# Gathered expert rows of a 32-row tile: weighting and adding them on GpSimd instead of DVE

## The chip, the cores and the metric

The kernel runs on one core of one Trainium2 chip. The metric is the device time of one execution in microseconds (us). The engines are named PE (TensorE, the matrix engine), DVE (VectorE), ACT (ScalarE), POOL (GpSimd) and SP (SyncE, here only a queue that starts transfers). DVE and POOL can both do elementwise work on tiles in SBUF; POOL cannot reach PSUM, where PE leaves its sums.

## What is computed

One inference step of a two-layer encoder. There are 288 tokens: 256 of a prompt and 32 of a sample. A layer is attention, a projection, a layer norm, a mixture of 16 experts of which each token uses two, and a second layer norm:

```python
x = layernorm(DN_ALPHA * x + mix, p['ln1_g'][l], p['ln1_b'][l])
ffn = grouped_moe(x, ...)   # y = y + gate[:, e:e + 1] * (h @ w_down[e])
x = layernorm(DN_ALPHA * x + ffn, p['ln2_g'][l], p['ln2_b'][l])
```

The change is in the last line of the second layer: `DN_ALPHA * x + ffn` for the sample's 32 rows. For each token `ffn` is the sum of two expert rows, each times its gate.

## The kernel before

Every engine has its own list of instructions, written out by hand in one function per engine; nothing reorders them. Semaphores are all that joins them: an instruction may wait for a count, and raises another when it is done. A helper `own(...)` raises the engine's own semaphore (or a named one), `own.settle()` waits for the last instruction that it issued, and `step(...)` does both on DVE.

Tokens lie on partitions in three tiles, `TOKS = [(0, P), (P, P), (2 * P, DEC)]`: tile 0 and tile 1 are the prompt (128 rows each), tile 2 is the sample (32 rows). `x_tok[:, t, :]` is tile t of the residual stream, 1024 values of float32 in each row.

In a layer, each expert works on a list of up to 64 tokens. PE multiplies them by the gate and up weights (`expert_up`, L916), DVE and ACT form the hidden values, PE turns them (`expert_turn`, L923) and multiplies by the down weights (`expert_down`, L930). The weights come in from HBM, 6 MB for each expert, through SP's queue. The results of the first 14 experts of the second layer are stored into the DRAM tensor `expert_rows` by ACT's queue (`store`, L1397). POOL's queue brings each token's two rows back with gathers (`bring_back`, L2043): for tile t the rows land in `back[0:n, s, t, :]`, with s = 0 and 1, and `back_in[t]` counts them. The six gathers are issued in the order tile 0, tile 1, tile 2. They start once the store of expert 13 has landed.

The last two experts of the second layer are not stored. ACT copies their results into `y_pair` (`keep`, L1405), and PE adds them to the tiles by a matmul with `pair_t`, a matrix with the tokens' gates. So the second layer ends like this:

- DVE multiplies `x_tok` by ALPHA in expert 14's time (L1868), and after expert 15's `turned` runs through the three tiles (L1934 to L1940). For each of a tile's two gathered rows one `scalar_tensor_tensor` computes `back * pair_gate + x_tok`, six of them in all. The second one of each tile raises `part_ready`.
- PE's `add_tile(l, t)` (L1021) waits for `part_ready` of tile t, puts the tile into PSUM with a matmul by the identity (L1026) and adds the last two experts' share (L1032). It raises `tile_ready`. Tiles 0, 1 and 2 have PSUM banks of their own (`sum_bank`).
- DVE's `combine(t)` (L1912) waits for `tile_ready` and computes the row statistics from PSUM (L1918, L1920), subtracts the mean and multiplies by the gain (L1923); ACT computes the root (L1359); DVE's `ln_finish` (L1725, L1727) multiplies by the inverse root and adds the offset. L1727 reads two tiles in SBUF, as L1939 does; L1923 reads one tile in PSUM and one in SBUF.
- SP stores each finished tile (L624).

The first layer has its own form of `combine` (L1926 to L1932) and ends without `add_tile`.

Of the kernel before, what the change touches and what calls it, by code (L numbers as in the profile page):

```python
# [21 lines left out]
ALU = mybir.AluOpType  # L22
# [4 lines left out]
SEQ, DEC, PAST, MEM = 256, 32, 256, 256  # L27
# [24 lines left out]
ALPHA = (2 * DEPTH) ** 0.25  # L52
# [54 lines left out]
def encoder_step(nc, ins, outs):  # L107
    ctx = ExitStack()
    with ctx:
        def sem(name):  # L110
            return ctx.enter_context(nc.semaphore(name))
# [24 lines left out]
        x_tok = base.cut(3, D)  # L136
# [23 lines left out]
        def cst(name, rows=slice(0, P)):  # L160
            a, n = CONST[name]
            return const[rows, a:a + n]
# [58 lines left out]
        back = Region(gu_one_at).cut(2, 3, D)  # L221
# [47 lines left out]
        pair_gate = zr.cut(2, 3)  # L269
# [45 lines left out]
        y_stored = [sem(f"y_stored{j}") for j in range(2)]  # L315
        back_in = [sem(f"back_in{t}") for t in range(3)]
        pair_ready = sem("pair_ready"); pair_turned = sem("pair_turned"); pair_taken = sem("pair_taken")
        pair_copied = sem("pair_copied"); part_ready = sem("part_ready"); tile_ready = sem("tile_ready")
        OV = ("ov_w", "ov_xg", "ov_gu", "ov_sig", "ov_h", "ov_ht", "ov_htc", "ov_y", "ov_yc", "ov_st", "ov_dve")
        ov = [{n: sem(f"{n}_{l}") for n in OV} for l in range(DEPTH)]  # L320
        out_mem = sem("out_mem"); out_kv = sem("out_kv"); out_dk = sem("out_dk"); out_y = sem("out_y")
# [97 lines left out]
        def pairs(l):  # L419

            return sum(PAIR[:l])

        def sum_bank(t, c):

            return bank[((0, 1), (5, 6), (2, 7))[t][c]]
# [212 lines left out]
        def rows_dst(i):  # L638

            blk, k0 = turns[i]  # L640
            a, n = ROW_BLOCKS[blk]
            return (xs[:, a:a + n, k0:k0 + 4].rearrange("p n k -> p k n"),
                    turn_bank(i)[:, :].rearrange("p (k n) -> p k n", k=4)[:, :, 0:n])
# [6 lines left out]
        def _(pe):  # L650
# [370 lines left out]
            def add_tile(l, t):  # L1021

                a, n = TOKS[t]
                pe.wait_ge(part_ready, 3 * pairs(l) + t + 1)
                for c in range(2):
                    mm(sum_bank(t, c)[0:n, :], ident[0:n, 0:n], x_tok[0:n, t, 512 * c:512 * c + 512], start=True, stop=False)  # L1026
                if t == 0:
                    pe.wait_ge(pair_taken, pairs(l) + 1)
                for c in range(2):
                    if t == 0:  # L1030
                        pe.wait_ge(pair_copied, 4 * pairs(l) + 3 + c)
                    last = mm(sum_bank(t, c)[0:n, :], pair_t[:, a:a + n], y_pair[:, c, :], start=False, stop=True)  # L1032
                last.then_inc(tile_ready, 1)
# [171 lines left out]
            for t in range(3):  # L1205
                add_tile(1, t)
# [289 lines left out]
        def _(ve):  # L1496
            own = Own(ve, dve_own)
            V = nc.vector
            tt, ts, stt, red = V.tensor_tensor, V.tensor_scalar, V.scalar_tensor_tensor, V.tensor_reduce

            def step(ins, s=None):

                own(ins, s)
                own.settle()
# [300 lines left out]
            def hidden(j, s, n, signal):  # L1805

                ts(act[:, j, :], act[:, j, :], 1.0, None, ALU.add).then_inc(s, 1)
                ve.wait_ge(s, n + 1)
                V.reciprocal(act[:, j, :], act[:, j, :]).then_inc(s, 1)
                ve.wait_ge(s, n + 2)  # L1810
                tt(act[:, j, :], act[:, j, :], bank[j][:, 0:256], ALU.mult).then_inc(s, 1)
                ve.wait_ge(s, n + 3)
                tt(hid[:, j, :], act[:, j, :], bank[j][:, 256:512], ALU.mult).then_inc(signal, 1)

            def hidden_t(j, signal):
                V.tensor_copy(hid_t[:, j].rearrange("p c n -> p (c n)"), bank[2][:, 0:256]).then_inc(signal, 1)  # L1816

            def experts(l):
                def form(e):

                    a = act[:, e % 2, :]
                    ve.wait_ge(sig_ready, NE * l + e + 1)
                    step(ts(a, a, 1.0, None, ALU.add))
                    step(V.reciprocal(a, a))  # L1824
                    step(tt(a, a, bank[e % 2][:, 0:256], ALU.mult))
                    own(tt(hid[:, e % 2, :], a, bank[e % 2][:, 256:512], ALU.mult), h_ready)

                def turned(e):
                    ve.wait_ge(ht_ready, NE * l + e + 1)
                    hidden_t(e % 2, ht_copied)  # L1830

                def pair_weights():

                    own(ts(pair_row, row_ab, float(-PAIR_ROW), None, ALU.add))
                    step(ts(pair_keep, row_ab, float(PAIR_ROW), None, ALU.is_ge))
                    step(stt(pair_keep, row_ab, float(ROWS), pair_keep, ALU.is_lt, ALU.mult))
                    step(ts(pair_keep, pair_keep, -1.0, 1.0, ALU.mult, ALU.add))
                    own(tt(row_ab, row_ab, pair_keep, ALU.mult))
                    step(tt(pair_gate, gates, pair_keep, ALU.mult))
                    own(V.tensor_copy(out_row[:, :], row_ab[:, :, :].rearrange("p s t -> p (s t)")))  # L1840
                    for t, (a, n) in enumerate(TOKS):
                        own(ts(pair_hot[0:n, t, :], cst("iota")[0:n], pair_row[0:n, 0, t:t + 1], gates[0:n, 0, t:t + 1],
                               ALU.is_equal, ALU.mult))
                        step(ts(pair_tmp[0:n], cst("iota")[0:n], pair_row[0:n, 1, t:t + 1], gates[0:n, 1, t:t + 1],
                                ALU.is_equal, ALU.mult))
                        step(tt(pair_hot[0:n, t, :], pair_hot[0:n, t, :], pair_tmp[0:n], ALU.add),
                             pair_ready if t == 2 else None)

                form(0)
                turned(0)  # L1850
                form(1)
                for i in range(1, TURNS, 2):
                    ve.wait_ge(rows_turned, TURNS * l + i + 1)
                    V.tensor_copy(*rows_dst(i)).then_inc(rows_taken["v"], 1)
                turned(1)
                form(2)
                for e in range(3, NE):
                    turned(e - 1)
                    form(e)
                    if PAIR[l] and e == 5:  # L1860
                        pair_weights()
                    if PAIR[l] and e == 7:
                        ve.wait_ge(pair_turned, pairs(l) + 1)
                        own(V.tensor_copy(pair_t, bank[5][:, 0:NT]), pair_taken)
                    if e == NE - 2:
                        ve.wait_ge(x_sorted, 96 * (l + 1))
                        for t in range(3):
                            own(ts(x_tok[:, t, :], x_tok[:, t, :], ALPHA, None, ALU.mult))  # L1868
                turned(NE - 1)
                ve.wait_ge(starts_ready, l + 1)  # L1870
                more = ve.value_load(flag[0:1, 0:1], min_val=0, max_val=1)
                with ve.If(more > 0):
                    o = ov[l]
                    with ve.Fori(0, NE) as e:
                        with ve.Fori(0, PASSES - 1) as q:
                            n = (PASSES - 1) * e + q
                            ve.wait_ge(o["ov_sig"], n + 1)
                            hidden(0, o["ov_dve"], 3 * (PASSES - 1) * e + 3 * q, o["ov_h"])
                            ve.wait_ge(o["ov_ht"], n + 1)
                            hidden_t(0, o["ov_htc"])  # L1880

            def after_attention(l):
# [21 lines left out]
                copies(f"xb{l}", lambda k, b: feat_dst(k + 2, b))  # L1904
                route(l)
                experts(l)

                own.settle()
# [23 lines left out]
                    ln_stats(2 * l + 1, t)  # L1932

                if PAIR[l]:  # L1934
                    for t in range(3):
                        n = TOKS[t][1]
                        ve.wait_ge(back_in[t], 32 * (l + 1))
                        for s in range(2):
                            step(stt(x_tok[0:n, t, :], back[0:n, s, t, :], pair_gate[0:n, s, t:t + 1], x_tok[0:n, t, :],  # L1939
                                     ALU.mult, ALU.add), part_ready if s else None)  # L1940
# [43 lines left out]
        def _(po):  # L1984
            own = Own(po, pool_own)
            G = nc.gpsimd
# [30 lines left out]
            def layer(l):  # L2017
# [34 lines left out]
                with po.If(more > 0):  # L2052
                    po.wait_ge(ov[l]["ov_st"], 32 * NE * (PASSES - 1))
                    ln_load(ln2_par, "ln2_g", "ln2_b", l)
                    bring_back(PASSES * ROWS)

            layer(0)
            layer(1)

# [1 line left out]
_INS = ["x_prompt", "x_sample", "cache_mla_ckv", "cache_mla_kpe", "cache_diff_k", "cache_diff_v", "cache_mem_k",  # L2061
# [25 lines left out]
```

## Time and profile before

| what | us |
|---|---|
| median of three runs | 941.51 |
| the three runs | 935.6, 941.51, 945.32 |
| the profiled execution, its own time | 942.3 |
| its span in the trace | 940.5 |
| PE busy | 807.9 (86% of the span) |
| DVE busy | 335.1 (36%) |
| POOL busy | 44.1 (5%), most of it the issuing of transfers |

The time of the profiled execution is 1.8 us above its span. All starts below are counted from the span's start. Shares of the whole span say little on this change: it lies in the last 25 us, so that stretch is what has to be read. Idle time of an engine counts only where the chain of waits runs through it.

### The profile page before, as it was taken

Reading aid. Unit: us, or ns where it says so; the run is one execution under the profiler, and the core shown is the slowest. Engines: PE = TensorE matmul, PEld = TensorE weight load, DVE = VectorE, ACT = ScalarE, POOL = GpSimd, SP = SyncE. Lnnn points to the kernel's source line nnn. Section 1 sums busy time; section 2 is a strip of 40 time slices with the busy share of each in tenths; the row PEclk is TensorE's granted clock in tenths of the full one; section 3 lists DMA queues with packets and bytes.
Section 4 is the critical chain, followed back from the end, with each engine's and each line's share of the span. In section 5 each row is a group of like instructions: output and inputs, shape, how many; then the busy total and the mean of one; then the engine's idle time right before and its main releaser. Section 6 shows DMA issues by size and latency. Waiting matters only on the chain.

```text
span 940.5 us, 10036 instructions
## 1 busy us (share of the span) xinstructions
PE 807.9 (86%) x3983; PEld 402.1 (43%) x3983; DVE 335.1 (36%) x749; ACT 186.5 (20%) x452; POOL 44.1 (5%) x58
## 2 busy tenths in 40 slices
PE   6979999998999887786889888879899998787875
PEld 4665777553433222222334566654544332222221
DVE  1025454444422221213360243454443342212138
ACT  1213343110311111100100034440103211101001
POOL 1012000002000000000200000000020000000020
PEclk9998899999999999998989897989999999999898
DMA  9624006746999999999596330093659999999991
GB/s 353 225 77 180 1 1 265 317 177 240 405 425 425 427 425 427 423 426 425 188 397 229 146 109 1 21 421 140 241 210 411 426 425 428 424 428 420 428 403 61
DMA packets 43553, 272.82 MB, mean 290 GB/s; under 512 B 6360, under 2 KB 11166, under 8 KB 25840
## 3 DMA queue, kind: packets, MB, share of 16 engines
q1 hardware_dynamic: 32032, 243.69, 63.0%
q0 software_dynamic: 5888, 19.95, 6.3%
q10 hardware_dynamic: 5584, 8.51, 2.5%
q8 instruction: 33, 0.54, 0.2%
q14 instruction: 16, 0.13, 0.0%
HBM read 253.92 MB, written 18.21 MB: 289 GB/s over the span
## 4 chain that ended last, share of the span: by engine, by line
PE 53%; DMA 26%; DVE 9%; SPq 6%; ACT 2%; issue 2%; POOL 0%; ACTq 0%; DVEq 0%; POOLq 0%
DMA arena<-in_expert_w_up 24%; PE bank L916 16%; PE bank L858 6%; PE bank L930 5%; PE bank L1176 5%; PE bank L845 3%; SPq L503 2%; PE bank L781 2%; PE bank L833 2%; PE bank L939 1%; PE bank L826 1%; PE bank L678 1%; PE bank L759 1%; PE bank L1141 1%; SPq L499 1%
## 5 line engine op out<-in xcount | busy, mean ns | idle before, releaser
L916 PE MATMUL bank<-arena 128*64 128x512 f32 x1024 | 240.8, 627 | 51.0 <-DMA arena<-in_expert_w_up 49.2
L916 PEld LDWEIGHTS bank<-arena 128*64 128x64 f32 x1024 | 77.2, 144 | 211.5 <-issue 148.2
L930 PE MATMUL bank<-arena 128*64 128x512 f32 x512 | 116.9, 598 | 16.7 <-DVE arena L1816 16.2
L1816 DVE COPY arena<-bank 128x256 f32<-128x256 f32 x32 | 13.6, 424 | 274.7 <-PE bank L923 274.7
L930 PEld LDWEIGHTS bank<-arena 128*64 128x64 f32 x512 | 34.1, 136 | 77.4 <-issue 55.4
L1372 ACT ACTIVATE arena<-bank 128x256 f32<-128x256 f32 x32 | 12.3, 384 | 268.8 <-PE bank L916 268.8
L1824 DVE RECIPROCAL arena<-arena 128x256 f32<-128x256 f32 x32 | 56.1, 1753 | 1.1
L858 PE MATMUL bank<-arena 128*128 128x512 f32 x128 | 56.0, 596 | 0.0
L1176 PE MATMUL bank<-arena 128*128 128x512 f32 x96 | 44.6, 628 | 5.0 <-DMA arena<-in_w_kv_shared 4.2
L845 PE MATMUL bank<-arena 128*128 128x288 f32 x128 | 39.0, 466 | 4.1 <-DVE arena L1964 4.1
L1234 ACT COPY arena<-bank 128x512 f32<-128x512 f32 (+2 forms) x30 | 15.8, 537 | 109.9 <-PE bank L678 71.7
L858 PEld LDWEIGHTS bank<-arena 128*128 128x128 f32 x128 | 24.0, 190 | 29.6 <-issue 29.5
L1394 ACT COPY arena<-bank 128x512 f32<-128x512 f32 x30 | 17.6, 587 | 91.1 <-PE bank L930 91.1
L845 PEld LDWEIGHTS bank<-arena 128*128 128x128 f32 x128 | 27.8, 223 | 13.1 <-issue 5.0
L1376 ACT COPY arena<-arena 128x512 f32 x28 | 31.4, 1127 | 8.5 <-issue 7.7
L1176 PEld LDWEIGHTS bank<-arena 128*128 128x128 f32 x96 | 19.2, 202 | 29.3 <-issue 23.9
L678 PE MATMUL bank<-arena 128*128 128x128 f32 (+1 forms) x144 | 23.9, 325 | 8.9 <-DVE arena L1979 3.2
L1517 DVE COPY arena<-bank 128x512 f32<-128x512 f32 (+3 forms) x20 | 12.9, 649 | 49.1 <-PE bank L678 17.6
L1049 PE MATMUL bank<-arena 128*128 128x512 f32 x64 | 28.0, 595 | 1.0 <-DVE arena L1517 1.0
L2015 POOL DMA_DIRECT2D arena<-in_ln_g x4 | 2.3, 567 | 560.3 <-ACT arena L1376 316.7
L678 PEld LDWEIGHTS bank<-arena 128*128 128x128 f32 (+1 forms) x144 | 22.0, 204 | 14.0 <-DVE arena L1979 4.2
L781 PE MATMUL bank<-arena 128*128 128x64 f32 (+1 forms) x172 | 26.1, 298 | 0.9 <-ACT arena L1328 0.7
(272 smaller groups left out, 889.1 us busy)
## 6 DMA issues: line engine op xcount, KB each, us to landing
arena<-in_expert_w_gate SPq DMA_DIRECT2D x32, 2048.0 KB, 22.5
arena<-in_expert_w_up SPq DMA_DIRECT2D x32, 2048.0 KB, 27.5
arena<-in_expert_w_down SPq DMA_DIRECT2D x64, 1024.0 KB, 30.9
arena<-in_w_out SPq DMA_DIRECT2D x4, 2048.0 KB, 9.7
expert_rows<-arena ACTq DMA_DIRECT2D x60, 128.0 KB, 7.9
arena<-in_w_kv_shared SPq DMA_DIRECT2D x3, 2048.0 KB, 10.4
arena<-in_w_mem_kv SPq DMA_DIRECT2D x2, 2048.0 KB, 21.4
arena<-sorted_rows POOLq DMA_DIRECT2D x2, 2048.0 KB, 9.2
```

The lines of the kernel that those rows point to most:

```text
L503: sp.dma_start(g_kv, ins["kv_norm_g"][0].partition_broadcast(P)).then_inc(small_in, 16)
L678: last = tr(b[:, k * n:(k + 1) * n], src[0:n, t, k0 + k::KC], ident[0:n, 0:n])
L781: last = mm(b[:, qt * w:(qt + 1) * w], pt[:, P * i:P * i + P], v[:, kt, h * w:(h + 1) * w], start=(i, kt) == mine_[0], stop=(i, kt) == min ...
L833: last = mm(b[:, 0:NT], w_q[:, k, 4 * g + hh, :], cq_feat[:, k, :], start=k == 0, stop=k == 2)
L845: last = mm(b[:, 0:NT], w_inb[k // 4][:, k % 4, P * c:P * c + P], x_feat[:, k, :], start=k == 0, stop=k == KC - 1)
L858: last = mm(b[:, :], x_feat[:, k, P * t:P * t + P], w_out[k // 4][:, k % 4, 512 * c:512 * (c + 1)], start=k == 0, stop=k == KC - 1)
L916: last = mm(bank[j][64 * half:64 * half + 64, :].rearrange("p (u f) -> p u f", u=2), slots[:, k, 0:CAP], w[:, :, k, 256 * half:256 * half ...
L930: last = mm(bank[3 + j][64 * n:64 * n + 64, :], hid_t[:, j, c, 64 * half:64 * half + 64], w[:, half, c, 512 * n:512 * n + 512], start=(hal ...
L1049: last = mm(b[:, :], feat[:, k, P * t:P * t + P], w[:, k, :], start=k == 0, stop=k == KC - 1)
L1176: last = mm(b[:, :], x_feat[:, k, P * t:P * (t + 1)], w_kvs[c][:, k, :], start=k == 0, stop=k == KC - 1)
L1376: return nc.scalar.copy(xg[:, j], xs[:, bass.ds(at, CAP), :].rearrange("p s k -> p k s"))
L1824: step(V.reciprocal(a, a))
```

## The change

The sample tile's two gathered rows are no longer weighted and added by DVE. POOL does it, in a new function `add_sample_rows(1)` behind everything else in POOL's program. Since POOL's program has no `scalar_tensor_tensor` here, each row takes two instructions, a `tensor_scalar` that multiplies `back` by the gate in place and a `tensor_tensor` that adds it to `x_tok`; each waits for the one before. POOL first waits for `back_in[2]` (the tile's gathers) and for `x_scaled`, a new semaphore that DVE raises when the multiplication by ALPHA (L1868) is done. The last addition raises `sample_part_ready`, and PE's `add_tile` waits for this one for tile 2. `part_ready` now counts two tiles. The first layer is as it was.

```diff
--- before.py
+++ after.py
@@ -315,7 +315,7 @@
         y_stored = [sem(f"y_stored{j}") for j in range(2)]
         back_in = [sem(f"back_in{t}") for t in range(3)]
         pair_ready = sem("pair_ready"); pair_turned = sem("pair_turned"); pair_taken = sem("pair_taken")
-        pair_copied = sem("pair_copied"); part_ready = sem("part_ready"); tile_ready = sem("tile_ready")
+        pair_copied = sem("pair_copied"); part_ready = sem("part_ready"); sample_part_ready = sem("sample_part_ready"); x_scaled = sem("x_scaled"); tile_ready = sem("tile_ready")
         OV = ("ov_w", "ov_xg", "ov_gu", "ov_sig", "ov_h", "ov_ht", "ov_htc", "ov_y", "ov_yc", "ov_st", "ov_dve")
         ov = [{n: sem(f"{n}_{l}") for n in OV} for l in range(DEPTH)]
         out_mem = sem("out_mem"); out_kv = sem("out_kv"); out_dk = sem("out_dk"); out_y = sem("out_y")
@@ -1021,7 +1021,10 @@
             def add_tile(l, t):
 
                 a, n = TOKS[t]
-                pe.wait_ge(part_ready, 3 * pairs(l) + t + 1)
+                if t < 2:
+                    pe.wait_ge(part_ready, 2 * pairs(l) + t + 1)
+                else:
+                    pe.wait_ge(sample_part_ready, pairs(l) + 1)
                 for c in range(2):
                     mm(sum_bank(t, c)[0:n, :], ident[0:n, 0:n], x_tok[0:n, t, 512 * c:512 * c + 512], start=True, stop=False)
                 if t == 0:
@@ -1865,7 +1868,7 @@
                     if e == NE - 2:
                         ve.wait_ge(x_sorted, 96 * (l + 1))
                         for t in range(3):
-                            own(ts(x_tok[:, t, :], x_tok[:, t, :], ALPHA, None, ALU.mult))
+                            own(ts(x_tok[:, t, :], x_tok[:, t, :], ALPHA, None, ALU.mult), x_scaled if t == 2 else None)
                 turned(NE - 1)
                 ve.wait_ge(starts_ready, l + 1)
                 more = ve.value_load(flag[0:1, 0:1], min_val=0, max_val=1)
@@ -1932,7 +1935,7 @@
                     ln_stats(2 * l + 1, t)
 
                 if PAIR[l]:
-                    for t in range(3):
+                    for t in range(2):
                         n = TOKS[t][1]
                         ve.wait_ge(back_in[t], 32 * (l + 1))
                         for s in range(2):
@@ -2054,8 +2057,20 @@
                     ln_load(ln2_par, "ln2_g", "ln2_b", l)
                     bring_back(PASSES * ROWS)
 
+            def add_sample_rows(l):
+
+                po.wait_ge(back_in[2], 32 * (l + 1))
+                po.wait_ge(x_scaled, l + 1)
+                for s in range(2):
+                    own(G.tensor_scalar(back[0:DEC, s, 2, :], back[0:DEC, s, 2, :], pair_gate[0:DEC, s, 2:3], None, ALU.mult))
+                    own.settle()
+                    own(G.tensor_tensor(x_tok[0:DEC, 2, :], x_tok[0:DEC, 2, :], back[0:DEC, s, 2, :], ALU.add),
+                        sample_part_ready if s else None)
+                    own.settle()
+
             layer(0)
             layer(1)
+            add_sample_rows(1)
 
 # ---- launch: one core; inputs and outputs as the reference has them ----
 _INS = ["x_prompt", "x_sample", "cache_mla_ckv", "cache_mla_kpe", "cache_diff_k", "cache_diff_v", "cache_mem_k",
```

Lines of the changed kernel are three higher than before from `add_tile` on: L1939 is L1942, L1918 is L1921, L1727 is L1730, L2043 is L2046.

The first place is DVE's program between the last expert and the first row statistics (`part_ready` and `back_in` are the semaphores named above, `dve_own` is DVE's own). Before:

```order
L1939 SCALAR_TENSOR_TENSOR arena<-arena 128x1024 [waits back_in0,h_ready]
L1939 SCALAR_TENSOR_TENSOR arena<-arena 128x1024 [waits dve_own]
L1939 SCALAR_TENSOR_TENSOR arena<-arena 128x1024 [waits back_in1,part_ready]
L1939 SCALAR_TENSOR_TENSOR arena<-arena 128x1024 [waits dve_own]
L1939 SCALAR_TENSOR_TENSOR arena<-arena 32x1024 [waits back_in2,part_ready]
L1939 SCALAR_TENSOR_TENSOR arena<-arena 32x1024 [waits dve_own]
L1918 BN_STATS arena<-bank 128x6 [waits tile_ready,part_ready]
L1918 BN_STATS arena<-bank 128x6
```

After:

```order
L1942 SCALAR_TENSOR_TENSOR arena<-arena 128x1024 [waits back_in0,h_ready]
L1942 SCALAR_TENSOR_TENSOR arena<-arena 128x1024 [waits dve_own]
L1942 SCALAR_TENSOR_TENSOR arena<-arena 128x1024 [waits back_in1,part_ready]
L1942 SCALAR_TENSOR_TENSOR arena<-arena 128x1024 [waits dve_own]
L1921 BN_STATS arena<-bank 128x6 [waits tile_ready,part_ready]
L1921 BN_STATS arena<-bank 128x6
```

The two additions of the 32-row tile are gone, and the row statistics of tile 0 stand right behind those of tile 1's additions.

The second place is the end of POOL's program, from the gathers of the second layer on. Before (the rows between the two branches are taken only where an expert has over 64 tokens, which is not so here):

```order
L2043 DMA arena<-expert_rows,out_row 128x1024 [waits y_stored1,y_stored0]
L2043 DMA arena<-expert_rows,out_row 128x1024 x3
L2043 DMA arena<-expert_rows,out_row 32x1024 x2
L2046 UNCONDITIONAL_BRANCH
L2052 COMPARE_AND_BRANCH
L2015 DMA arena<-in_ln_g 128x1024 [waits ov_st_1]
L2015 DMA arena<-in_ln_b 128x1024
L2043 DMA arena<-expert_rows,out_row 128x1024 x4
L2043 DMA arena<-expert_rows,out_row 32x1024 x2
L2052 UNCONDITIONAL_BRANCH
```

After:

```order
L2055 UNCONDITIONAL_BRANCH
L2065 ISA
L2065 TENSOR_SCALAR arena<-arena 32x1024 [waits x_scaled,back_in2]
L2067 TENSOR_TENSOR arena<-arena 32x1024 [waits pool_own]
L2065 TENSOR_SCALAR arena<-arena 32x1024 [waits pool_own]
L2067 TENSOR_TENSOR arena<-arena 32x1024 [waits pool_own]
L109 UNCONDITIONAL_BRANCH [waits sample_part_ready]
```

Four elementwise instructions on 32x1024 stand behind the gathers. Ahead of them is a row that the program before has nowhere, `ISA` of L2065. In the built program it is a request to reload GpSimd's code library; it waits for no semaphore.

## Rows read from the trace of the kernel before

**Rows 1.** The page: the span.

```profile
span 940.5 us, 10036 instructions
```

**Rows 2.** The chain that ended last, 880 to 941: start us, us, what.

```profile
902.18 8.78 PE bank L916 x32
...
916.41 0.18 DVEq L1871
...
917.35 1.30 DVE arena L1939
...
923.94 1.28 DVE arena L1939
...
925.25 1.31 DVE arena L1918 x2
...
936.87 1.28 DVE arena L1727
```

**Rows 3.** Timeline 890 to 941: start us, us, engine, line, op.

```profile
920.11 1.98 PE L1026 MATMUL bank<-arena 128*128 128x512 f32 x4
920.22 1.19 ACT L1405 COPY arena<-bank 64x512 f32<-64x512 f32 x2 [3.42 <-PE bank L930]
921.42 1.28 ACT L1359 ACT_TABLE_LOAD   x1
...
921.93 1.88 PE L1032 MATMUL bank<-arena 128*128 128x512 f32 x4
...
927.17 1.90 PE L1026 MATMUL bank<-arena 32*32 32x512 f32 x4
...
928.34 1.29 DVE L1727 SCALAR_TENSOR_TENSOR arena<-arena 128x1024 f32<-128x1024 f32 x1
929.00 1.90 PE L1032 MATMUL bank<-arena 128*32 128x512 f32 x4
...
929.54 1.29 DVE L1918 BATCH_NORM_STATS2 arena<-bank 128x6 f32<-128x512 f32 x2
...
933.83 1.28 DVE L1918 BATCH_NORM_STATS2 arena<-bank 32x6 f32<-32x512 f32 x2
...
938.18 0.33 SPq L624 DMA_DIRECT2D out_y_sample<-arena  x1
```

**Rows 4.** Timeline of POOL: the last gather of tile 2.

```profile
913.37 0.86 POOL L2043 DMA_INDIRECT arena<-expert_rows,out_row  x1 [0.30 <-issue]
```

**Rows 5.** DMA issues, 913.3 to 914.2: count, median us from issue to landing.

```profile
arena<-expert_rows,out_row POOLq DMA_INDIRECT x1, 6.1
```

**Rows 6.** Groups of POOL's instructions: busy us, mean ns of one, idle before.

```profile
L2003 POOL COPY arena<-arena 128x3456 f32<-128x3456 f32 x1 | 3.1, 3062 | 41.8 <-DMA arena<-in_w_uq 41.8
...
L2003 POOL COPY arena<-arena 128x576 f32<-128x576 f32 x2 | 1.3, 659 | 0.0
```

**Rows 7.** Timelines of POOL (61.2 to 64.2) and DVE (60.5 to 66).

```profile
61.25 3.06 POOL L2003 COPY arena<-arena 128x3456 f32<-128x3456 f32 x1 [41.80 <-DMA arena<-in_w_uq]
...
63.65 0.74 DVE L1543 TENSOR_TENSOR arena<-arena 128x64 f32<-128x64 f32 x1 [29.73 <-DMA arena<-in_lambda_k]
...
64.67 0.32 DVE L1543 TENSOR_TENSOR arena<-arena 128x64 f32<-128x64 f32 x1
```

**Rows 8.** Three lines by themselves: ns min/median/max, first and last start.

```profile
L2010 POOL COPY arena<-arena x7: 641/651/876, 73.1 to 77.0; 64x544 f32<-64x544 f32 x7
...
L1578 DVE SCALAR_TENSOR_TENSOR arena<-arena x3: 774/776/821, 75.0 to 76.6; 128x288 f32<-128x288 f32 x3
...
L1551 DVE SCALAR_TENSOR_TENSOR arena<-arena x3: 479/479/485, 65.5 to 66.3; 128x256 f32<-128x256 f32 x3
```

**Rows 9.** Windows: length, busy PE, PEld, DVE, ACT, POOL, granted clock, DMA share, GB/s.

```profile
898.00:902.20 4.20, 0.02 (x2) 0.02 (x2) 0.81 (x2) 0.51 (x1) 0.00 (x0) 1.00 0.96 404
902.20:906.40 4.20, 4.20 (x12) 1.30 (x14) 0.00 (x0) 0.00 (x0) 0.00 (x0) 0.59 1.04 427
...
931.00:934.00 3.00, 0.00 (x0) 0.00 (x0) 2.93 (x6) 0.29 (x1) 0.00 (x0) 0.93 0.25 101
```

## Prediction, made before the changed kernel ran

> **What bounds the kernel now.** I read the span first [rows 1], then the chain of waits over its last 60 us [rows 2], since the change touches only instructions there. To see in it: up to 916 the chain is expert work (PE's L916 at 902.18), and from 917.35 to the end every step is DVE's. Six additions of L1939 come first, 1.32 us from start to start ((923.94 - 917.35) / 5), then three equal rounds of row statistics and finish, one for each tile. DVE never waits in them. So whatever DVE does not have to do before 925.25 can shorten the kernel, until another engine ends last. The timeline says which one that is [rows 3].
>
> **What the change removes.** DVE loses two additions, 2 x 1.32 = 2.64 us on the chain. With four left DVE is free at 917.35 + 4 x 1.32 = 922.6. But the statistics of tile 0 also need PE's sum. PE's identity matmuls for tile 0 start at 920.11, and its L1032 starts at 921.93 and takes 1.88, so it ends at 923.81 [rows 3]. That was hidden behind the fifth and sixth addition and is now late next. The statistics start at 923.85 instead of 925.25. The gain is 1.40 us, not 2.64.
>
> A round takes (933.83 - 925.25) / 2 = 4.29 us [rows 2, 3]. Without further waits tile 2's statistics are wanted at 923.85 + 8.58 = 932.43. PE needs 3.73 us for tile 2 (from 927.17 to 929.00 + 1.90 [rows 3]), so to keep the whole gain POOL has to be done at 928.7. If it is done later than 933.83 - 3.73 = 930.1, the kernel is slower than before for this reason alone.
>
> **What the change adds: POOL's start.** The last gather of tile 2 is issued at 913.37 [rows 4] and lands 6.1 us after issue, at 919.5 [rows 5]. The wait for `x_scaled` is free: the ALPHA multiplication lies in expert 14's time, some 20 us before. Between the last gather (over at 914.23) and the new work POOL passes its branches. DVE's own took 916.41 to 917.35, 0.94 us [rows 2], so POOL gets to the reload of its code library at 915.2. No row shows what the reload costs. The low end is nothing; a neighbour of it is ACT's table load of 1.28 us [rows 3]. The high end is 6.1 us, the time of a small transfer from issue on POOL's queue to landing [rows 5]. I take 6.1, since code has to come from memory as the gathered rows do. So POOL begins at 921.3, and at 919.5 if the reload is short. Nothing else is queued behind on POOL; only PE's tile 2 waits for it.
>
> The GPSIMD Engine Reference of the Trainium skill (section Instruction dispatch) gives about 6 us before the first call to a freshly loaded kernel, without an instruction in the profile. No row here shows it; the sum would stay as it is.
>
> **POOL's four instructions.** POOL's copies show its rate with one input: 3062 ns for 3456 values and 659 for 576 [rows 6], which is 0.834 ns a value and 0.18 us fixed, so 1.03 us for 1024. I take this for the multiplication. 32 rows cost what 128 do, as a row is read along its length. For the addition, with two inputs, no row stands in the trace. It costs at least 1.03, and with each input streamed in turn 0.18 + 2 x 0.85 = 1.89. I take 1.89, because only the streaming with one input has a row and there are two to stream. In all 2 x (1.03 + 1.89) = 5.8, with four waits of some 0.03 us 6.0 us; the low bound is 4.2. Undisturbed POOL would go from 921.3 to 927.3, before 928.7, and the gain of 1.40 would stand.
>
> **It is not undisturbed.** At 63.65 a DVE `tensor_tensor` of only 64 values took 0.74 us; it ended at 64.39, just after POOL's copy (61.25 + 3.06 = 64.31). Its twin at 64.67 took 0.32 [rows 7]. While POOL's seven copies of 544 values ran, three DVE additions of 288 values took 0.774 to 0.821 us each, where the same operation on 256 took 0.479 without POOL; POOL's copies rose from 0.641 to 0.876 [rows 8]. All those DVE instructions read two tiles in SBUF. So the two engines take turns, an instruction each. The Trainium skill says the same (SBUF — State Buffer, section SBUF: two separate sides): the loser of the shared ports blocks fully, and DVE instructions with two SBUF inputs are concerned. By that rule, the trace agrees.
>
> In the tail L1939 and L1727 read two SBUF tiles. Turn by turn from 921.3: multiplication to 922.3; DVE's fourth addition 922.3 to 923.6, which is 1.0 late but still before tile 0's sum at 923.85, so free (PE is busy with tile 0 until 923.8 anyhow); addition to 925.5; multiplication to 926.5; addition to 928.5. Meanwhile DVE comes to L1727 of tile 0 at 928.34 - 1.40 = 926.94 [rows 3] and waits until 928.5, 1.56 us. That wait is on the chain. PE's tile 2 is then ready at 928.5 + 3.73 = 932.2, in time. Sum: - 1.40 + 1.56 = + 0.2 us.
>
> With a free reload POOL starts at 919.95, behind DVE's second addition. It delays the third by 1.0 and the fourth by 1.9, so tile 0's statistics start at 925.4, and it is done before DVE's L1727. Sum: + 0.15. The result hardly hangs on the reload as long as that is at most 6 us: DVE gets rid of two additions, and POOL's turns take the time back.
>
> The GPSIMD reference (section Performance versus the Vector engine) measures a two-input addition of 2048 values at 4497 ns, an estimate of 2.25 us for 1024. No row shows one. With it the last addition would end at 929.2, L1727 would wait 2.3 us, and the sum would be + 0.9.
>
> **Against the measured times.** The profiled execution took 942.3 (span 940.5 plus 1.8 outside it), 0.8 above the median of 941.51. The sum gives 942.5 for such an execution and 941.7 for the median.
>
> **Rivals.**
> - **POOL's turns take the gain back** (forecast, chance 0.47): + 0.2, between - 0.3 and + 0.9 with the other prices. 941.7.
> - **The gain stands** (0.18): POOL's instructions fall between DVE's, or take less than 1.89, and DVE does not wait at L1727: - 1.40, 940.1. Against it stand [rows 7, 8]; for it, that DVE's additions of the tail need only 5 of the 8 us in question and that row statistics and L1923 read PSUM, beside which POOL is free.
> - **POOL is late** (0.35), the case on the slower side. The mechanism is the reload ahead of the first multiplication, and the point is 930.1: each us beyond it is a us of the kernel. With a reload 3 us longer POOL starts at 924.3, lets L1727 of tile 0 in between, ends about 931.4, and the kernel is 1.3 slower. With 12 us it starts at 927.2 and ends at 934.5 or so: 4.4 slower. Then PE has stood idle from 927.2 for 7 us. Its granted clock fell from 1.00 to 0.59 (so to 1.2 GHz for most of the stretch) in 902.20 to 906.40, behind an idle stretch of 4.2 us, and began to fall at the end [rows 9]; PE's 3.73 us would double, 8 slower in all. This case gives 942.2 to 949.5, most likely 943. Over 9.4 us, that is 1%, only with a reload of about 13 us or more: 0.03.
> - **The move does nothing at all** would need DVE to be off the chain, which the chain excludes [rows 2].
>
> **How the numbers follow.** The forecast is 941.7. The cases span - 1.4 to + 8, with nine parts in ten between - 1.4 and + 3. The three runs shown lie 5.9 below and 3.8 above their median, more than any likely effect, so the spread of runs makes most of the range: a median of a few runs moves by some 4 us either way, upward with the late case added. Range 936.5 to 947. About 1% is what a measurement of this kernel can tell from no change. No case is 1% faster; 0.03 for the spread. Slower 0.05: the late case's far end and the spread. Within 1%: 0.92.
>
> **What would show it.** Right: four L1942 instructions; L1921 of tile 0 at 1.3 to 1.5 us before its old place; POOL's L2065 first at about 921; L2067 near 1.9 us; one L1730 stretched from 1.29 towards 2.8 us; PE's L1029 of tile 2 right behind POOL's last. The gain stands if no L1942 and no L1730 is longer than 1.3. POOL is late if L1921 of tile 2 waits for PE. Wrong in the base of it: DVE waiting nowhere while POOL runs beside L1942 or L1730, or L2065 before 919.5.

## The result: slower by 0.7%

| | before | changed |
|---|---|---|
| median of 12 runs, us | 941.15 | 945.63 |
| lowest and highest | 935.6, 946.04 | 938.35, 951.39 |
| profiled execution's span | 940.5 | 949.3 |

The ratio of changed to before is 1.0067, with a 95% interval of 1.0038 to 1.0097: slower by 3.6 to 9.1 us, where 941.7 and a loss of 0.2 were forecast. (The two medians by themselves are 4.5 us apart.) The measured time lies inside the range given, but a loss of this size, clear of the noise, is that of the rival that said POOL is late.

Of the 8.8 us between the two spans 4.4 lie ahead of the place that was changed: DVE's first gathered addition starts at 917.35 in the one profile and at 921.78 in the other. Across the profiles of the kernels below, whose work up to there is nearly the same, it starts between 913.3 and 923.1, so nothing ties this half to the change. So all that follows is counted from that first addition. From it to the end of the last L1727 (now L1730) pass 20.8 us before and 25.1 us now: 4.3 us, which lies inside the interval; what the ratio's 6.3 us have beyond that is not explained here.

### The profile after

The chain that ended last, as start us, us, what, from the last gather on. It answers to the DVE steps of [rows 2]:

```profile
915.97 7.95 DMA arena<-expert_rows,out_row
...
924.02 3.10 POOL arena L2065
...
927.18 2.78 POOL arena L2067
...
930.06 2.84 POOL arena L2065
...
932.97 2.34 POOL arena L2067
...
935.36 3.62 PE bank L1029 x4
938.98 3.57 PE bank L1035 x4
...
942.57 1.30 DVE arena L1921 x2
```

Before, every step behind 917.35 was DVE's. Now the chain leaves DVE: the gather (it lands at 923.92), POOL's four instructions, PE's tile 2, and only then DVE. POOL's four take 935.31 - 924.02 = 11.3 us. PE's tile 2 takes 7.2 us where it took 3.73 [rows 3].

The timeline of the same stretch (start us, us, engine, line, op, and the idle time ahead) answers to [rows 3]:

```profile
921.78 5.98 DVE L1942 SCALAR_TENSOR_TENSOR arena<-arena 128x1024 f32<-128x1024 f32 x4 [0.89 <-issue]
...
928.34 1.30 DVE L1921 BATCH_NORM_STATS2 arena<-bank 128x6 f32<-128x512 f32 x2 [0.58 <-PE bank L1035]
...
931.43 1.28 DVE L1730 SCALAR_TENSOR_TENSOR arena<-arena 128x1024 f32<-128x1024 f32 x1
...
935.36 3.62 PE L1029 MATMUL bank<-arena 32*32 32x512 f32 x4 [3.69 <-POOL arena L2067]
...
942.57 1.29 DVE L1921 BATCH_NORM_STATS2 arena<-bank 32x6 f32<-32x512 f32 x2 [5.56 <-PE bank L1035]
```

Four additions take 5.98 us instead of 4 x 1.32; the third one took 2.02. It costs nothing, because DVE waits for PE's tile 0 anyway (0.58). Tile 0's statistics start 6.56 us after the first addition, where they started 7.90 after it: the gain of 1.34 is there. L1730 of tile 0 takes 1.28 and is not stretched. The loss is in tile 2 alone: its statistics start 20.8 us after the first addition instead of 16.5, and DVE idles 5.56 us for them.

Windows of the same stretch (length; busy us and count of PE, PEld, DVE, ACT, POOL; granted clock; DMA share; GB/s) answer to [rows 9]:

```profile
928.10:931.70 3.60, 3.57 (x9) 1.30 (x7) 3.25 (x7) 0.29 (x1) 3.50 (x2) 1.00 0.00 0
931.70:934.10 2.40, 0.00 (x0) 0.00 (x0) 2.37 (x4) 0.00 (x0) 2.32 (x2) 1.00 0.22 90
934.10:935.30 1.20, 0.00 (x0) 0.00 (x0) 1.16 (x3) 0.29 (x1) 1.20 (x1) 0.55 0.63 256
935.30:942.50 7.20, 7.14 (x8) 1.05 (x8) 1.67 (x3) 0.00 (x0) 0.01 (x1) 0.50 0.18 73
```

PE finishes tile 1 at 931.7 and has nothing to do until POOL is done at 935.3. During this idle time the granted clock falls from 1.00 to 0.50, from 2.4 GHz to 1.2 GHz, and stays there through all of tile 2's matmuls: 0.50 in the last window, where they take 7.2 us.

So the trace splits the 4.3 us in three. DVE's gain is - 1.34; by it alone tile 2's statistics would start at 15.1. POOL ends at 13.5 us, 3.7 us after PE was ready for it at 9.9; had PE kept its clock, the statistics would start near 17.3. POOL's lateness so costs 2.2 us, the gain of 1.34 and 0.8 to 0.9 more. The clock adds 7.2 - 3.73 = 3.5 us.

### The profile page after: what moved, and what is told of

It is laid out like the page before. It is cut to its first block, busy times and chain, and to the rows that moved or that the text cites. A ratio compares the mean times of both kernels' runs of the same rounds, so it can differ in the third digit from the quotient of the medians.

```text
span 949.3 us, 10041 instructions
## 1 busy us (share of the span) xinstructions
PE 816.2 (86%) x3983; PEld 404.9 (43%) x3983; DVE 333.8 (35%) x747; ACT 186.3 (20%) x452; POOL 55.1 (6%) x62
## 4 chain that ended last, share of the span: by engine, by line
PE 53%; DMA 27%; DVE 7%; SPq 6%; ACT 2%; POOL 2%; issue 2%; ACTq 0%; DVEq 0%; POOLq 0%
DMA arena<-in_expert_w_up 23%; PE bank L916 15%; PE bank L858 6%; PE bank L1179 5%; PE bank L930 5%; PE bank L845 3%; SPq L503 2%; PE bank L781 2%; PE bank L833 2%; PE bank L685 2%; DMA arena<-expert_rows,out_row 1%; PE bank L678 1%; PE bank L826 1%; PE bank L939 1%; PE bank L759 1%
## 5 line engine op out<-in xcount | busy, mean ns | idle before, releaser
L1827 DVE RECIPROCAL arena<-arena 128x256 f32<-128x256 f32 x32 | 56.1, 1753 | 1.1
L858 PE MATMUL bank<-arena 128*128 128x512 f32 x128 | 56.0, 595 | 0.0
L1179 PE MATMUL bank<-arena 128*128 128x512 f32 x96 | 44.4, 625 | 5.7 <-DMA arena<-in_w_kv_shared 4.8
L678 PE MATMUL bank<-arena 128*128 128x128 f32 (+1 forms) x144 | 24.3, 331 | 8.7 <-DVE arena L1982 3.2
L1052 PE MATMUL bank<-arena 128*128 128x512 f32 x64 | 30.7, 642 | 1.0 <-DVE arena L1520 1.0
L685 PE MATMUL bank<-arena 128*128 128x128 f32 (+1 forms) x68 | 27.9, 513 | 0.0
```

Source lines behind the costliest of these rows:

```text
L678: last = tr(b[:, k * n:(k + 1) * n], src[0:n, t, k0 + k::KC], ident[0:n, 0:n])
L685: mm(b[:, 0:n], ident, const[:, 0:n], start=True, stop=True)
L858: last = mm(b[:, :], x_feat[:, k, P * t:P * t + P], w_out[k // 4][:, k % 4, 512 * c:512 * (c + 1)], start=k == 0, stop=k == KC - 1)
L1052: last = mm(b[:, :], feat[:, k, P * t:P * t + P], w[:, k, :], start=k == 0, stop=k == KC - 1)
L1179: last = mm(b[:, :], x_feat[:, k, P * t:P * (t + 1)], w_kvs[c][:, k, :], start=k == 0, stop=k == KC - 1)
```

## Experiments

Five of the eight were timed against the kernel before in 12 runs each. Three ran once, under the profiler: the quiet probe (942.6 us), the rate probe (946.2) and the one with writes alone (948.1). The intervals are about 0.35% either way, or 3.3 us, so effects of 1 us are read from the traces and not from the times.

| kernel | ratio to before (95%) | tile 2's statistics start | last L1730 ends |
|---|---|---|---|
| before | 1 | 16.5 | 20.8 |
| changed | 1.0067 (1.0038 to 1.0097) | 20.8 | 25.1 |
| additions left out | 0.9999 (0.9965 to 1.0032) | 15.1 | 19.5 |
| PE kept busy | 1.0028 (0.9992 to 1.0064) | 17.4 | 21.7 |
| sample's gathers first | 1.0030 (0.9997 to 1.0063) | 17.8 | 22.1 |
| ACT multiplies | 1.0014 (0.9978 to 1.0050) | 15.4 | 19.8 |
| one row each | 1.0003 (0.9971 to 1.0034) | 16.1 | 20.5 |
| POOL only writes | one run | 19.6 | 23.9 |
| quiet probe | one run | 20.8 | 25.1 |
| rate probe | one run | 21.7 | 26.0 |

The last two columns are us after DVE's first gathered addition, in the profiled run. The two probes hold the whole change and add work to POOL only ahead of the gathers; the quiet one repeats the changed kernel's tail to the tenth. My theory after the result (A): POOL is late through its own slowness, and PE, idle for it, loses its clock. The rivals: another place got slower (B); PE's tile 2 is slow for another reason than its clock (C); the reload of POOL's library holds it (D); DVE and POOL hold each other up (A2).

### The additions left out

```diff
-            add_sample_rows(1)
...
-                    pe.wait_ge(sample_part_ready, pairs(l) + 1)
+                    pe.wait_ge(x_scaled, l + 1)
```

> The sample tile's two additions are left out altogether (its output lacks the experts that were gathered); PE's tile 2 waits only for the multiplication by ALPHA. Theory A (POOL is late, and the idle PE loses its clock): with POOL gone from the end the whole gain of 1.4 us against before stands, because PE's tile 0 is what the first row statistics wait for: they begin 6.5 us after DVE's first addition, tile 2's 15.1 us after it (16.5 before, 20.8 in the changed kernel). Ratio to before 0.998. Rival B (something else at the end or before it got slower, such as the lost PE sum or the SP queue): the time stays 3 to 5 us above before.

Measured: 0.9999 (0.9965 to 1.0032). DVE's rows:

```profile
917.79 5.25 DVE L1942 SCALAR_TENSOR_TENSOR arena<-arena 128x1024 f32<-128x1024 f32 x4 [0.89 <-issue]
924.35 1.30 DVE L1921 BATCH_NORM_STATS2 arena<-bank 128x6 f32<-128x512 f32 x2 [1.31 <-PE bank L1035]
...
932.93 1.28 DVE L1921 BATCH_NORM_STATS2 arena<-bank 32x6 f32<-32x512 f32 x2
```

Tile 0's statistics start 6.56 after the first addition and wait 1.31 us for PE, tile 2's at 15.1. The whole gain that the move can bring is 1.3 us of 941, and even with the work left out it does not show in the times. Rival B asked for 3 to 5 us above before and is out: the interval ends at + 3.0 us, and in the trace nothing of the 4.3 us is left without POOL's four instructions.

### PE kept busy while it waits

```diff
                 else:
+                    keep_warm(bank[3], 2048)
                     pe.wait_ge(sample_part_ready, pairs(l) + 1)
```

> The changed kernel, with four 512-column matmuls into an unused bank (3.4 us at the clock granted before) on PE between tile 1 and its wait for POOL. Theory A: the granted clock stays at 1.00 through PE's tile 2, whose eight matmul pieces take 3.7 us instead of 7.2; POOL ends as late as before; the kernel is 3.5 us faster than the changed one and 0.8 us slower than before (ratio 1.001). Rival C (POOL's lateness alone is the cost, PE's tile 2 is slow for another reason, such as POOL's writes or 32-row matmuls): the clock or the 7.2 us do not change, and the time stays at the changed kernel's, ratio 1.005 or more.

Measured: 1.0028 (0.9992 to 1.0064). This interval holds what A expected (1.001) as well as what C expected (1.005), so the times do not decide; the trace does. PE's rows of the timeline, and a window over tile 2 (columns as above):

```profile
927.99 3.60 PE L685 MATMUL bank<-arena 128*128 128x512 f32 x8
931.85 1.90 PE L1030 MATMUL bank<-arena 32*32 32x512 f32 x4 [0.26 <-POOL arena L2068]
933.68 1.91 PE L1036 MATMUL bank<-arena 128*32 128x512 f32 x4
```

```profile
931.70:935.70 4.00, 3.73 (x8) 0.70 (x8) 1.83 (x4) 0.00 (x0) 0.09 (x1) 1.00 0.32 131
```

L685 is the filling work. POOL ends at 13.5 us after the first addition, as in the changed kernel, but the clock stays at 1.00 and tile 2 takes 3.7 us. Its statistics start at 17.4 instead of 20.8: 3.4 us are the clock's, 0.9 is the loss against before that stays. As theory A had it; rival C is out.

### Writes instead of POOL's arithmetic

```diff
-                for s in range(2):
-                    own(G.tensor_scalar(back[0:DEC, s, 2, :], back[0:DEC, s, 2, :], pair_gate[0:DEC, s, 2:3], None, ALU.mult))
...
+                for n in range(11):
+                    own(G.memset(back[0:DEC, 0, 2, :], 0.0), sample_part_ready if n == 10 else None)
+                    own.settle()
```

> POOL's four instructions are replaced by eleven memsets of one gathered row (so the sample tile's output lacks the gathered experts), about 11 us in all. Theory A (the granted clock falls because PE idles, whatever POOL does): POOL ends near 13.4 us after DVE's first addition, no DVE addition is stretched, PE idles 3.5 us, its clock is 0.50 through tile 2's matmuls and they take 7.2 us; tile 2's statistics begin at about 20.7. Rival (POOL's reads and adds, or its writes to the tile that PE loads, slow PE): the matmuls take 3.7 us.

```profile
926.30:929.90 3.60, 3.60 (x9) 1.33 (x7) 3.15 (x7) 0.29 (x1) 3.37 (x5) 1.00 0.00 0
929.90:932.40 2.50, 0.07 (x1) 0.00 (x0) 2.46 (x4) 0.00 (x0) 2.39 (x3) 1.00 0.22 88
932.40:939.50 7.10, 6.96 (x8) 1.06 (x8) 2.84 (x5) 0.29 (x1) 0.09 (x1) 0.52 0.29 117
```

POOL was done at 12.4, a little earlier than meant, and PE idled 2.57 us only. The clock still was 0.52 over tile 2's 7.1 us. None of DVE's additions was stretched (all 1.285 us). So the clock is lost without any of POOL's reads and arithmetic, and in the kernel above it is kept with all of them: it is PE's idleness that costs it.

### POOL's instructions by themselves

```diff
...
+                        own(G.memset(probe, 1.0))
+                        own(G.memset(back[:, 0, 0, :], 0.0))
+                        own.settle()
+                        for n in (DEC, DEC, P):
+                            own(G.tensor_scalar(probe[0:n, :], probe[0:n, :], back[0:n, 0, 0, 0:1], None, ALU.mult))
+                            own.settle()
+                            own(G.tensor_tensor(back[0:n, 0, 0, :], back[0:n, 0, 0, :], probe[0:n, :], ALU.add))
+                            own.settle()
```

> The changed kernel, with two extra pairs of multiplication and addition on 32x1024 and one pair on 128x1024 on POOL in expert 14's time, when DVE is nearly idle. Theory A1 (POOL's instructions are slow by themselves): a multiplication takes 2.5 to 2.8 us and an addition 2.3 alone, on 32 rows as on 128. Rival A2 (POOL's instructions are short, and DVE's instructions with two SBUF inputs held them up): a multiplication takes 1.0 to 1.5 us alone and an addition 2.3; the 2.8 to 3.1 at the end are waits. The gap between the last memset and the first multiplication shows the reload: 6 to 7 us if the reload is a real cost that the gather had hidden, under 1 if not.

POOL's rows in the quiet stretch (busy us, mean ns of one, idle before), two from its timeline, and the records of the reload (count, ns, start us):

```profile
L2058 POOL TENSOR_SCALAR arena<-arena 32x1024 f32<-32x1024 f32 x2 | 5.7, 2838 | 0.2
L2060 POOL TENSOR_TENSOR arena<-arena 32x1024 f32<-32x1024 f32 x2 | 4.7, 2345 | 0.2
L2058 POOL TENSOR_SCALAR arena<-arena 128x1024 f32<-128x1024 f32 x1 | 2.9, 2854 | 0.1
L2060 POOL TENSOR_TENSOR arena<-arena 128x1024 f32<-128x1024 f32 x1 | 2.6, 2650 | 0.1
```

```profile
877.25 0.98 POOL L2055 MEMSET arena<- 128x1024 f32 x1
878.34 2.85 POOL L2058 TENSOR_SCALAR arena<-arena 32x1024 f32<-32x1024 f32 x1
```

```profile
L2058 POOLq MODIFY_POOL_CONFIG  x2: 54/54/54, 878.2 to 878.2; - x2
```

A1 holds for 32 rows: a multiplication takes 2.84 us and an addition 2.35 with nothing beside them. Two of each are 10.4 us. Of the 11.3 in the changed kernel 0.9 are waits and the gaps between instructions (3.09 and 2.77 for the first two), the rest is POOL's own speed. On 128 rows the multiplication takes the same. The addition's 2.65 was not measured alone: DVE's multiplication by ALPHA ran from 891.75 to 892.48, and POOL's addition began at 892.02. The reload stands between the memset's end (878.23) and 878.34: 0.1 us. A reload of 6 to 7 us would have shown here, so rival D is out. (In the changed kernel its records stand at 916.8, 7 us ahead of the first multiplication, while POOL waited for the gather.)

### What makes the multiplication slow

```diff
...
+                        p, b = probe[0:DEC, :], back[0:DEC, 0, 0, :]
+                        for make in (lambda: G.tensor_copy(p, b), lambda: G.tensor_scalar(p, b, 2.0, None, ALU.mult),
+                                     lambda: G.tensor_scalar(p, b, back[0:DEC, 0, 1, 0:1], None, ALU.mult),
+                                     lambda: G.tensor_scalar(p[:, 0:512], b[:, 0:512], 2.0, None, ALU.mult),
+                                     lambda: G.tensor_tensor(p[:, 0:512], p[:, 0:512], b[:, 0:512], ALU.add)):
+                            own(make())
+                            own.settle()
```

> The changed kernel with a row of POOL instructions on 32 partitions in a stretch where DVE is nearly idle: a copy of 1024 values, a multiplication by a constant, one by a value for each partition into another tile, a multiplication by a constant of 512 values, an addition of 512. Theory A: all arithmetic on POOL is slow, copy and memset are not: copy 1.0 us, both multiplications 2.8, the one of 512 values 1.5, the addition of 512 1.3. Rival (the multiplication is slow for its per-partition factor, or for writing in place): the constant one takes about 1.1 us, or the one into another tile does.

```profile
882.17 1.03 POOL L2058 COPY arena<-arena 32x1024 f32<-32x1024 f32 x1
883.29 2.79 POOL L2058 TENSOR_SCALAR arena<-arena 32x1024 f32<-32x1024 f32 x1
886.19 2.83 POOL L2059 TENSOR_SCALAR arena<-arena 32x1024 f32<-32x1024 f32 x1
889.11 1.48 POOL L2060 TENSOR_SCALAR arena<-arena 32x512 f32<-32x512 f32 x1
890.68 1.25 POOL L2061 TENSOR_TENSOR arena<-arena 32x512 f32<-32x512 f32 x1
```

The copy of 1024 values takes 1.03 us, to the hundredth what [rows 6] gave. The multiplication takes 2.7 times that, with a constant (2.79) as with a factor for each partition (2.83). Both write into another tile, so writing in place is not the reason either. The copy's rate does not carry over to arithmetic.

### The sample's gathers first

```diff
-                    for t, (a, n) in enumerate(TOKS):
+                    for t, (a, n) in [(t, TOKS[t]) for t in ((2, 0, 1) if PAIR[l] else (0, 1, 2))]:
```

> The changed kernel, with the second layer's gathers of tile 2 issued ahead of those of tiles 0 and 1. Theory A: POOL can begin 2 to 2.5 us earlier and still needs 11.3 us (up to 1.5 more, because more of DVE's additions stand beside it), so its last addition ends about 11.5 us after DVE's first addition instead of 13.5. PE then idles 1.6 us instead of 3.7 and keeps its clock: tile 2's statistics come at 15.2 to 16 us after DVE's first addition, ratio to before 0.998 to 1.000. Rival D (the library reload holds POOL's start, not the gather): the first multiplication does not begin earlier, being about 7 us behind the last gather's issue, and the time stays at the changed kernel's.

Measured: 1.0030 (0.9997 to 1.0063), tile 2's statistics at 17.8; the expectation of 15.2 to 16 was wrong. POOL:

```profile
912.58 2.85 POOL L2065 TENSOR_SCALAR arena<-arena 32x1024 f32<-32x1024 f32 x1 [1.62 <-DMA arena<-expert_rows,out_row]
915.51 2.35 POOL L2067 TENSOR_TENSOR arena<-arena 32x1024 f32<-32x1024 f32 x1
917.96 3.70 POOL L2065 TENSOR_SCALAR arena<-arena 32x1024 f32<-32x1024 f32 x1
921.74 2.79 POOL L2067 TENSOR_TENSOR arena<-arena 32x1024 f32<-32x1024 f32 x1
```

DVE's first, second and fourth additions, and the statistics of tile 0 and 2, in timelines of their own windows:

```profile
916.42 2.52 DVE L1942 SCALAR_TENSOR_TENSOR arena<-arena 128x1024 f32<-128x1024 f32 x1 [0.88 <-issue]
...
918.98 2.02 DVE L1942 SCALAR_TENSOR_TENSOR arena<-arena 128x1024 f32<-128x1024 f32 x1
...
922.36 3.25 DVE L1942 SCALAR_TENSOR_TENSOR arena<-arena 128x1024 f32<-128x1024 f32 x1
925.64 1.30 DVE L1921 BATCH_NORM_STATS2 arena<-bank 128x6 f32<-128x512 f32 x2
...
934.23 1.28 DVE L1921 BATCH_NORM_STATS2 arena<-bank 32x6 f32<-32x512 f32 x2
```

POOL started 3.8 us before DVE's first addition instead of 2.2 behind it, and PE no longer idled at the end. But now the additions met. DVE's took 2.52, 2.02, 1.285 and 3.25 us, tile 0's statistics start at 9.2 instead of 6.6, and PE's tiles 0 and 1 come later too. Being early trades the late tile 2 for a DVE that is held up: here the forecast's own mechanism does take the gain back, and 1.3 us more.

### ACT multiplies, POOL adds

```diff
                 experts(l)
+                if PAIR[l]:
+                    ac.wait_ge(back_in[2], 32 * (l + 1))
+                    for s in range(2):
+                        own(nc.scalar.mul(back[0:DEC, s, 2, :], back[0:DEC, s, 2, :], pair_gate[0:DEC, s, 2:3]), sample_weighted)
...
                 for s in range(2):
-                    own(G.tensor_scalar(back[0:DEC, s, 2, :], back[0:DEC, s, 2, :], pair_gate[0:DEC, s, 2:3], None, ALU.mult))
-                    own.settle()
+                    po.wait_ge(sample_weighted, s + 1)
```

> The changed kernel, with ACT instead of POOL multiplying the two gathered rows by their gates (about 1.1 us each, after its copies for expert 15); POOL keeps the two additions. Theory A (POOL's own speed made it late, 2.84 us a multiplication and 2.34 an addition, and lateness then cost PE its clock): ACT is done 6.2 us after DVE's first addition, POOL at 10.0 instead of 13.5, PE does not idle, its clock holds, no DVE addition is stretched, L1730 of tile 0 waits about 0.3 us. Tile 2's statistics begin at 15.4 (before 16.5, changed kernel 20.8): 1 us faster than before, ratio 0.999. Rival (any use of POOL beside DVE's additions costs DVE what it saves): DVE's instructions are stretched and tile 2's statistics begin at 16.5 or later.

Measured: 1.0014 (0.9978 to 1.0050). From the timelines of POOL, DVE and PE:

```profile
928.51 4.77 POOL L2069 TENSOR_TENSOR arena<-arena 32x1024 f32<-32x1024 f32 x2 [6.53 <-ACT arena L1473]
...
923.13 5.25 DVE L1946 SCALAR_TENSOR_TENSOR arena<-arena 128x1024 f32<-128x1024 f32 x4 [0.89 <-issue]
...
932.78 1.58 DVE L1734 SCALAR_TENSOR_TENSOR arena<-arena 128x1024 f32<-128x1024 f32 x1
...
938.56 1.28 DVE L1925 BATCH_NORM_STATS2 arena<-bank 32x6 f32<-32x512 f32 x2
...
933.33 1.90 PE L1029 MATMUL bank<-arena 32*32 32x512 f32 x4 [0.31 <-POOL arena L2069]
```

Each step came as expected: POOL ends 10.2 us after the first addition, PE idles 0.31 us and keeps its clock, DVE's one collision costs 0.3 us (L1734 takes 1.58), tile 2's statistics start at 15.4. The tail is 1.0 us shorter than before's; the times cannot tell that from nothing, and their middle lies on the slower side (1.0014).

### One row on DVE, one by ACT and POOL

ACT multiplies row s = 0 as in the kernel above; besides that:

```diff
+                    ve.wait_ge(back_in[2], 32 * (l + 1))
+                    own(stt(x_tok[0:DEC, 2, :], back[0:DEC, 1, 2, :], pair_gate[0:DEC, 1, 2:3], x_tok[0:DEC, 2, :],
+                            ALU.mult, ALU.add), sample_one)
...
+                po.wait_ge(sample_weighted, 1)
+                po.wait_ge(sample_one, 1)
+                own(G.tensor_tensor(x_tok[0:DEC, 2, :], x_tok[0:DEC, 2, :], back[0:DEC, 0, 2, :], ALU.add), sample_part_ready)
```

> Of the sample tile's two rows DVE weights and adds one, as its fifth addition; ACT weights the other one, and POOL only adds it, behind DVE's fifth addition. Theory A: five additions end when PE's sum of tile 0 is ready (6.56 us after the first), so nothing of the gain of 1.3 us is lost to the fifth; POOL's one addition runs from 6.6 to 9.0, between DVE's fifth addition and L1730 of tile 0, so it stretches nothing; PE's tile 2 follows tile 1 without a gap. Tile 2's statistics begin at 15.2, ratio 0.9986, the most that can be had as long as PE's tile 0 comes first. Rival (POOL's turn beside the row statistics costs too): L1921 or L1926 is longer than 0.70 and 0.75 us.

Measured: 1.0003 (0.9971 to 1.0034), tile 2's statistics at 16.1 instead of 15.2. POOL's one addition (2.34 us) stretched nothing, as expected, but in this profile DVE had to wait twice for gathers of the prompt tiles:

```profile
919.05 2.60 DVE L1946 SCALAR_TENSOR_TENSOR arena<-arena 128x1024 f32<-128x1024 f32 x2 [2.53 <-DMA arena<-expert_rows,out_row]
922.78 2.60 DVE L1946 SCALAR_TENSOR_TENSOR arena<-arena 128x1024 f32<-128x1024 f32 x2 [1.13 <-DMA arena<-expert_rows,out_row]
```

The wait of 1.13 us inside the additions is what is missing from the gain. The wait ahead of them is not in the table at all: 2.53 us where the other profiles have 0.89, so the point from which the columns count is itself 1.6 us late, and from the end of DVE's copy of expert 15 (916.52) to the end of the last L1734 (939.52) this kernel took 23.0 us, where the one before took 21.7 (916.46 to 938.15). The gathers were in time in the other profiles; how often they are not stays open. No version here is shown to beat the kernel before.

## Why the prediction was wrong, step by step

- **The gain at DVE's end: right.** 1.40 forecast, 1.34 measured, with PE's tile 0 as what is late next.
- **POOL's start: 1.7 us earlier than forecast.** I had it 3.95 us after DVE's first addition, by a reload of 6.1 us. It started at 2.2, as soon as the gather had landed; the reload costs 0.1 us in the quiet probe. This error alone would have helped. The Trainium skill (GPSIMD Engine Reference, section Instruction dispatch) has about 6 us for a freshly loaded kernel; the quiet probe does not show it here.
- **POOL's four instructions: the step that failed.** The prediction had 2 x (1.03 + 1.89) and 6.0 us in all. Alone they take 2 x (2.84 + 2.35) = 10.4, in the kernel 11.3. Most of the error is the multiplication, which I priced as the nearest row, a copy with one input [rows 6]; it takes 2.84 instead of 1.03. The bounds were wrong too: twice the streaming was taken as the top for two inputs, and no top at all was set for one. The estimate of 2.25 us for the addition, worked out from the Trainium skill (GPSIMD Engine Reference, section Performance versus the Vector engine), was near (2.35).
- **The point from which it decides: right, and passed.** POOL ended at 13.5 us after the first addition; the prediction's point was 930.1 - 917.35 = 12.75. Beyond it each us costs a us: 0.8.
- **The clock: seen as part of a rival, but only for a long reload; the sum had no term for it.** I had it fall after 7 us of idling, going by a stretch in which 4.2 us had passed at 1.00 [rows 9]. Here it fell at 934.2, 2.5 us after PE's last matmul and ahead of all of tile 2, so the length of an idle stretch alone does not tell when it falls. This is the largest term, 3.5 of the 4.3 us. The last window of [rows 9] had the nearer row; I named it ("began to fall at the end") and drew nothing from it. In the kernel before PE ends tile 2 at 930.90, and the clock fell 2.7 us later; it cost nothing there, as no matmul was left:

```profile
933.40:933.60 0.20, 0.00 (x0) 0.00 (x0) 0.20 (x1) 0.00 (x0) 0.00 (x0) 0.99 0.00 0
933.60:933.80 0.20, 0.00 (x0) 0.00 (x0) 0.20 (x1) 0.00 (x0) 0.00 (x0) 0.50 0.00 0
```

- **Turns at L1727, the forecast's + 1.56: did not happen.** L1730 of tile 0 stood inside POOL's second multiplication (930.06 to 932.89) and took 1.28. A multiplication held DVE up only near its start: the third addition by 0.73 us, which PE's tile 0 hid; and in the rate probe, where POOL was later and the second multiplication began 0.5 us ahead of it, tile 0's L1730 (there L1731) by 0.42 us. The kernel with the sample's gathers first shows where the turns matter: an addition of POOL's held DVE's fourth for 2.0 us.

The forecast's time of 941.7 came from a balance of - 1.40 and + 1.56. The first term measured - 1.34. The second measured nothing; in its place stand 2.2 us of PE's wait for POOL and 3.5 of its clock. The rival "POOL is late" had the place, the point and the clock, and gave up to 949.5; I gave it 0.35 and tied it to the reload, where a wrong price of the arithmetic sufficed.

## What to carry to other kernels

Price work that is moved to another engine by a row of the same operation on that engine; a copy's rate is no rate for arithmetic. Then ask who waits at the new place and what that engine does meanwhile: a PE that idles ahead of its last matmuls can lose more by its clock than by the wait, as here with 3.5 us against 2.2. And before any of it, bound the whole gain by the engine that is late next: here 1.3 us in 941, less than these runs can show, against a risk several times as large.

## What the runs showed of the hardware

- POOL took 2.84 us for `tensor_scalar` and 2.35 for `tensor_tensor` on 32x1024 float32, and 1.03 for a copy of the same size; `tensor_scalar` was slower than the addition with two inputs. On 512 values they took 1.48 and 1.25. `tensor_scalar` on 128 rows took 2.85.
- POOL and DVE exclude each other unevenly. An addition of POOL's held a DVE instruction that reads two tiles in SBUF nearly to its end (waits of 1.2 and 2.0 us in the kernel with the sample's gathers first), a multiplication by 0.7 us at most. In the quiet probe additions of POOL's also held DVE `tensor_scalar` instructions with one tile in SBUF: L1872 took 2.82 us instead of 0.69, L1827 1.22 instead of 0.28. In the tail DVE's instructions that read PSUM (L1921, L1926) were never stretched, nor was any beside POOL's memsets. The Trainium skill (SBUF — State Buffer, section SBUF: two separate sides) has the shared ports held for a whole instruction; for the addition the runs agree, for the multiplication they do not: L1730 ran its 1.28 us wholly inside one of 2.83 us.
- PE's granted clock went from 1.00 to 0.50 in an idle stretch of 3.7 us in the changed kernel, and at the end of one of 2.6 us in the kernel with writes alone. Over the 7 us of matmuls that followed it was 0.50 and 0.52. With filling matmuls in the gap it stayed at 1.00.
- From the records of the library reload to POOL's first arithmetic 0.1 us passed, in the quiet probe (878.2 to 878.34) and in the rate probe (883.2 to 883.29).
